# Queries and values by seven block products, and two parts of the modulation summed later

## The chip, the cores and the metric

The kernel runs on one core of a Trainium2 chip. What counts is the device time of one execution in microseconds, as the median of several runs. The times shown are 3068.38 us as median of three runs (3064.83 to 3071.08). The profile is of one further execution, which took 3069.78 us with a span of 3067.9 us from the first to the last instruction.

## The reference

Two residual blocks follow each other on 256 tokens of width 2048, all in float32. The change touches the first one only:

```
mod   = silu(c) @ w_mod + b_mod              # 6 parts of 2048
hl    = modulate(rms_norm(x), mod[0], mod[1])    # 256 tokens
hc    = modulate(rms_norm(ctx), ...)             # 256 context tokens
zl    = hl @ w_in + b_in        # conv, gating (su, sv), q, k, v, 3 gates
zkv   = hc @ w_in[k, v] + b_in
y_na  = neighbourhood_attention(q, k, v, kc, vc, rpb)
x     = x + mod[2] * (g_conv*y_conv + g_sgu*y_sgu + g_att*y_att) @ w_o
h2    = modulate(rms_norm(x), mod[3], mod[4])
x     = x + mod[5] * (square(relu(h2 @ w_ff1 + b1)) @ w_ff2 + b2)
```

q needs the 256 tokens only; k and v need the tokens and the context. `mod[2]` to `mod[5]` are vectors of 2048: each is a sum over 2048 rows of `w_mod` weighted by `silu(c)`. The second block has its own projections, a dilated attention and three recurrences, and is not touched.

## The kernel before

**Engines and queues.** The order of the work is written out by hand for each engine, in one function per engine, with semaphores between them. TensorE (PE) does all products, VectorE (DVE) the element work, ScalarE (ACT) activations and copies out of PSUM. SyncE's queue (SP) loads the weights into a ring of four slots of 1 MB, in the order of the table `STREAM`; a slot is loaded again once PE has released it. The queue of GpSimd (POOL) loads the chunks of `w_mod`.

**Two kinds of product.** A stationary product (`one_slot`, line 473) goes through the slot's 128 columns: sixteen matmuls with 256 tokens (q, su, sv) or 512 (k). The other kind is `pair` (line 493): the block of 256 columns by 256 tokens is cut in halves on the three axes, and seven products of the halves replace eight. Three of the seven read the ring directly. The other four read sums of weight blocks, which DVE makes in `pair_differences` and `pair_sums` (lines 1773, 1754, 1785) and announces on `weight_sums`; `quarter_sums` (line 1815 on) makes the sums of the inputs, announced on `input_sums`. `add_products` (lines 1797 to 1806, five operations) puts the seven results together and frees the two PSUM banks. There is one buffer `TX` for the weight sums: the differences of the next pair wait for `differences_used`, its first sum for the first bank of the pair before to be full, its second sum for the second bank, which is full when PE has done the pair. The three gates' projections and most of the feed-forward layers are done so.

**The stages around the change.** After the opening PE does su, sv, q, k and v, then gate_conv, the output projections of conv and sgu, gate_sgu and gate_att (16 pairs, called gate_sgu below), out_att, the output projection, ff1 and ff2. In q each of eight slots is a stationary product; in k too, with layer norm sums of the other branches between; v is done with the tokens as the stationary operand, 128 products of 512 columns (line 770). The attention itself is spread through the gate stages.

**The modulation.** Each of parts 3 to 6 (here called first to fourth, `mod_columns(0)` to `(3)`) is summed by DVE over sixteen chunks of 128 rows by 2048 columns (`add_chunk`, line 1918) into `MACC`, and a small product of PE (`mod_sum`, line 684) sums it over the partitions; it waits on `mod_added`. Two buffers hold chunks, and the table `CHUNK_AT` says beside which slot a chunk's load may start. All 64 chunks are added between the end of the opening and the end of v: twenty between the 24 groups of eleven convolution taps (line 1970), the others around the layer norms and during v.

Of the kernel before, what the change touches and what calls it, by code (L numbers as in the profile page):

```python
# [18 lines left out]
ALU = mybir.AluOpType  # L19
# [37 lines left out]
for _n, _pack in enumerate(PACKS):  # L57
# [10 lines left out]
    ("q", "w_in", WQ, 2, 16, 128), ("k", "w_in", WK, 2, 16, 128), ("v", "w_in", WV, 2, 4, 512),  # L68
# [38 lines left out]
def second_layer(q):  # L107
# [7 lines left out]
CHUNK_PARTS = tuple(g for g in range(24) if g not in (10, 11, 12, 20))  # L115
CHUNK_AT = (-4, -3, 0, 1, 2, 3, *(3 + g for g in CHUNK_PARTS), *(x - 12 for x in (39, 39, 39, 40, 40, 40, 42, 42, 42, 43, 43, 43, 44, 44, 44, 45, 45, 45,
            46, 46, 46, 47, 48, 48, 48, 48, 49, 49, 49, 49, 50, 50, 50, 50, 51, 51, 51, 51)))
assert len(CHUNK_AT) == 64

# [42 lines left out]
def program(nc, dram, out):  # L162
    ctx = ExitStack()
    with ctx:
# [17 lines left out]
        glw = sb("glw", [P, KT, 32])  # L182
        small = sb("small", [P, 16])
# [43 lines left out]
        MACC_ROWS = at(34032, KT, 4, 32)  # L227
# [18 lines left out]
        XS, X21 = at(24592, 7, HT, P), at(13328, HT, P)  # L246
        TB, TB0 = [at(o, 4, HT, P) for o in (4096, 14352)]
# [11 lines left out]

        TO = [at(2048 * e, 4, 4, P) for e in range(2)]  # L260
# [106 lines left out]
        def _(sp):  # L367
# [58 lines left out]
        def _(pe):  # L426
# [57 lines left out]
            def pair(p, x, tb, mid=None, first=0, tokens=False):  # L484
# [21 lines left out]
                for i, t, o in ((0, 3, psum[:, b, P:2 * P]), (1, 5, psum[:, b, 2 * P:3 * P]),  # L506
# [6 lines left out]
                    if i == 1:  # L513
                        mm.then_inc(sem("differences_used"), n["differences_used"].up())
                    elif i == 2:
                        mm.then_inc(sem(full("dve", a)), n[full("dve", a)].up())
                    elif i == 3:
                        mm.then_inc(sem(full("dve", b)), n[full("dve", b)].up())

# [159 lines left out]
            def mod_sum(b):  # L679
# [3 lines left out]
                for i in range(4):  # L683
                    mm = pe.matmul(psum[32 * i:32 * i + 32, b, :], ones[:, 0:32], MACC_ROWS[:, :, i, :], start=True,
                                   stop=True)
# [15 lines left out]

            def ahead_of_sv(q, k):
                if q == 5 and k == 0:
                    mod_sum(7)
# [54 lines left out]
            for half in range(2):  # L759
                for t in range(4):  # L760
                    take(4 * half + t, "act")
                for s in range(4):
                    w = slot(s, 512)
                    for k in range(4):
                        for t in range(4):
                            if half == 0 and s == k == 1 and t == 0:
                                mod_sum(7)
                            elif half == 1 and s == 3 and k == 2 and t == 0:
                                mod_sum(3)
                            mm = pe.matmul(psum[:, 4 * half + t, :], H[:, 4 * s + k, t * P:(t + 1) * P], w[:, k, :],  # L770
                                           start=(s == k == 0), stop=(s == k == 3))
                            if t == k == 0:
                                leave(mm, s)
                            if s == k == 3:
                                mm.then_inc(sem(full("act", 4 * half + t)), n[full("act", 4 * half + t)].up())


# [44 lines left out]
            pe.wait_ge(sem("input_sums"), n["input_sums"].next())  # L822
# [109 lines left out]
            for q in range(64):  # L932
                hidden_slot(q)

# [248 lines left out]
        def _(act):  # L1183
# [113 lines left out]
            def beside_su(q):  # L1297
# [7 lines left out]
                elif q < 6:  # L1305
# [7 lines left out]
                    if q == 5:  # L1313
                        settled("ctx_normed", range(4, 6))

            beside("su", tiles("su", ZU, ACT.Gelu_apprx_tanh, (cols, COL["b_in"] + SU // P)), beside_su)
            beside("sv", tiles("sv", ZV, ACT.Gelu_apprx_tanh, (cols, COL["b_in"] + SV // P)), alone)
            settled("uv_ready")
            act.wait_ge(sem("bq_ready"), n["bq_ready"].next())
            beside("q", lambda i, s: A(turned(one(NQ, i * 4 + s)), psum[:, s, 0:T].rearrange("p (r c) -> p r c", c=GRID),  # L1320
                                       ACT.Identity, scale=0.125, bias=bq[:, ds(i * 4 + s, 1)]), alone)

            def beside_k(q):
                if q == 4:

                    load(kept[0], at(0, 4096), "load_x_out")
# [14 lines left out]
            for half in range(2):  # L1341
                for t in range(4):
                    b = 4 * half + t
                    act.wait_ge(sem(full("act", b)), n[full("act", b)].next())
                    A(NV[:, t, half * 512:half * 512 + 512], psum[:, b, :], ACT.Copy).then_inc(
                        sem(free("act", b)), n[free("act", b)].up())
            settled("qkv_ready", range(8))
# [243 lines left out]
        def _(pool):  # L1591
# [39 lines left out]
            for j in range(64):  # L1631
# [18 lines left out]

            pool.wait_ge(sem("gates_added"), n["gates_added"].next())
# [23 lines left out]
            pool.dma_start(kept[1], at(36080, 4096)).then_inc(sem("load_tables_out"), 16)  # L1675
# [1408 lines left out]
```

## Time and profile before

| | |
|---|---|
| median of three runs | 3068.38 us |
| the profiled execution | 3069.78 us, span 3067.9 us |
| PE busy | 3016.4 us, 98% |
| DVE busy | 2056.0 us, 67% |
| ACT, POOL busy | 332.4 us, 63.2 us |
| mean granted clock of TensorE | 0.998 |
| q stage (from about 324 us), v stage | eight slots up to 379.5 us; 500.35 to 612.67 us |
| gate_sgu and gate_att, last pairs | up to 1066.0 us |
| ff1 pairs, second layer | from 1246.9 us; from 1626.3 us |

An engine's busy share is a mean over stages with different limits. PE is busy almost throughout from 170 us on, so the time of a stage is what PE has to do in it plus what it waits, and DVE's idle time in a stage says how much more it could take there before PE feels it. A matmul in float32 shows as two records in the trace, so 16 products are x32.

### The profile page before, as it was taken

How to read it: one execution, taken by the hardware profiler on the slowest of the kernel's cores; microseconds unless marked ns; L12 is line 12 of the kernel's file. 1: busy time of each engine (PE TensorE's matmuls, PEld its weight loads, DVE VectorE, ACT ScalarE, POOL GpSimd, SP SyncE). 2: the span in 40 equal slices, each digit the busy share in tenths (PEclk: the TensorE clock that was granted, in tenths of full speed). 3: DMA queues.
4: the chain of work that ended last, by engine and by line, in shares of the span. 5: the costliest groups of instructions: out<-in, count | busy, mean ns of one | idle time of the engine just before them, and what ended most of it. 6: DMA issues, size and time to landing. Idle time of an engine off the chain costs nothing.

```text
span 3067.9 us, 50576 instructions
## 1 busy us (share of the span) xinstructions
PE 3016.4 (98%) x22131; PEld 2727.2 (89%) x22143; DVE 2056.0 (67%) x3101; ACT 332.4 (11%) x651; POOL 63.2 (2%) x121
## 2 busy tenths in 40 slices
PE   6899999999999999999999999999999999999998
PEld 3588844499999999999999999999999998898998
DVE  1039975567876577766756777877667566996665
ACT  1011000023220000111110000001012102001010
POOL 0000000120000000000000000000000000000000
PEclk9999999999999999999999999999999999999999
DMA  8899977664445555755555555565444654553443
GB/s 290 289 310 297 295 241 287 227 186 137 138 138 165 182 176 165 190 168 165 192 173 165 169 166 165 166 174 172 148 145 146 206 174 124 154 140 110 124 151 111
DMA packets 580137, 561.45 MB, mean 183 GB/s; under 512 B 24317, under 2 KB 548176, under 8 KB 570445
## 3 DMA queue, kind: packets, MB, share of 16 engines
q1 hardware_dynamic: 550368, 466.65, 49.7%
q0 software_dynamic: 11552, 80.90, 7.1%
q10 hardware_dynamic: 17997, 10.67, 1.2%
q8 instruction: 175, 2.87, 0.4%
q14 instruction: 45, 0.37, 0.0%
HBM read 549.66 MB, written 8.51 MB: 182 GB/s over the span
## 4 chain that ended last, share of the span: by engine, by line
PE 73%; DVE 1%; issue 0%; ACT 0%; DVEq 0%; ACTq 0%
PE psum L493 36%; PE psum L473 15%; PE psum L571 2%; PE psum L901 2%; PE psum L891 2%; PE psum L903 2%; PE psum L896 2%; PE psum L893 2%; PE psum L902 2%; PE psum L888 2%; PE psum L536 2%; PE psum L946 1%; PE psum L529 1%; PE psum L583 1%; PE psum L1076 0%; PE psum L1089 0%
## 5 line engine op out<-in xcount | busy, mean ns | idle before, releaser
L473 PE MATMUL psum<-arena,ring 128*128 128x256 f32 (+2 forms) x3200 | 756.1, 397 | 0.9 <-ACTq L1191 0.9
L473 PEld LDWEIGHTS psum<-arena,ring 128*128 128x128 f32 x3200 | 604.2, 190 | 138.8 <-issue 63.5
L493 PE MATMUL psum<-arena 128*128 128x128 f32 x6144 | 702.8, 275 | 0.3 <-DVE arena L1785 0.3
L493 PEld LDWEIGHTS psum<-arena 128*128 128x128 f32 x6144 | 694.4, 192 | 7.2 <-issue 6.2
L493 PE MATMUL psum<-arena,ring 128*128 128x128 f32 x4224 | 486.1, 275 | 0.0
L493 PEld LDWEIGHTS psum<-arena,ring 128*128 128x128 f32 x4224 | 479.1, 192 | 0.7 <-issue 0.5
L1773 DVE TENSOR_TENSOR arena<-ring 128x2048 f32<-128x2048 f32 x96 | 220.0, 2292 | 278.4 <-PE psum L493 276.0
L1918 DVE SCALAR_TENSOR_TENSOR arena<-arena,cvec 128x2048 f32<-128x2048 f32 x60 | 141.0, 2350 | 78.6 <-DMA arena<-w_mod 77.7
L1754 DVE TENSOR_TENSOR arena<-ring,arena 128x1024 f32<-128x1024 f32 (+1 forms) x184 | 178.3, 969 | 5.7
L1754 DVE TENSOR_TENSOR arena<-arena 128x512 f32<-128x512 f32 (+7 forms) x267 | 141.2, 529 | 16.3 <-DVE arena L2696 5.7
L2553 DVE TENSOR_TENSOR arena<-ring 128x1024 f32<-128x1024 f32 x64 | 78.4, 1225 | 90.3 <-PE psum L888 89.5
L1785 DVE TENSOR_TENSOR arena<-ring,arena 128x1024 f32<-128x1024 f32 x96 | 117.6, 1225 | 3.6 <-DVE arena L1754 0.3
L770 PE MATMUL psum<-ring,arena 128*128 128x512 f32 x256 | 110.6, 593 | 1.0 <-ACT arena L1339 1.0
L633 PE MATMUL psum<-arena,ring 128*128 128x256 f32 x448 | 104.8, 389 | 6.7 <-DMA ring<-w_in 4.3
L633 PEld LDWEIGHTS psum<-arena,ring 128*128 128x128 f32 x448 | 85.3, 194 | 28.9 <-DMA ring<-w_in 16.6
L770 PEld LDWEIGHTS psum<-ring,arena 128*128 128x128 f32 x256 | 48.4, 190 | 63.2 <-issue 63.2
L891 PE MATMUL psum<-arena,ring 128*128 128x128 f32 x512 | 99.0, 275 | 0.0
L901 PE MATMUL psum<-arena 128*128 128x128 f32 x512 | 99.0, 275 | 0.0
L893 PE MATMUL psum<-arena,ring 128*128 128x128 f32 x512 | 99.0, 275 | 0.0
L902 PE MATMUL psum<-arena 128*128 128x128 f32 x512 | 99.0, 275 | 0.0
L903 PE MATMUL psum<-arena 128*128 128x128 f32 x512 | 99.0, 275 | 0.0
L888 PE MATMUL psum<-arena,ring 128*128 128x128 f32 x512 | 99.0, 275 | 0.0
(345 smaller groups left out, 3211.8 us busy)
## 6 DMA issues: line engine op xcount, KB each, us to landing
ring<-w_ff SPq DMA_DIRECT2D x128, 1024.0 KB, 5.7
ring<-w_in SPq DMA_DIRECT2D x88, 1024.0 KB, 7.3
arena<-w_mod POOLq DMA_DIRECT2D x64, 1024.0 KB, 6.6
ring<-ab_w_in SPq DMA_DIRECT2D x56, 1024.0 KB, 5.7
ring<-cd_w_in SPq DMA_DIRECT2D x48, 1024.0 KB, 5.8
ring<-w_mod SPq DMA_DIRECT2D x32, 1024.0 KB, 7.6
ring<-w_in SPq DMA_DIRECT2D x32, 512.0 KB, 4.8
ring<-w_o SPq DMA_DIRECT2D x16, 1024.0 KB, 5.8
```

The source lines that it names most:

```text
L473: mm = pe.matmul(psum[:, s, m * N:(m + 1) * N], w[:, k, m * P:(m + 1) * P], x(k)[:, 0:N], start=(j == 0), stop=(j == kt - 1))
L493: return pe.matmul(o, z, w, **kw) if tokens else pe.matmul(o, w, z, **kw)
L633: mm = pe.matmul(psum[:, b, m * T:(m + 1) * T], w[:, k, m * P:(m + 1) * P], HL[:, 4 * g + k, :], start=False, stop=g == 3 and k == 3 and m ...
L770: mm = pe.matmul(psum[:, 4 * half + t, :], H[:, 4 * s + k, t * P:(t + 1) * P], w[:, k, :], start=(s == k == 0), stop=(s == k == 3))
L888: mm = pe.matmul(psum[:, a, 0:P], quarters(s, 0, 0)[:, j], HID[:, 8 * g + 2 * j, 0:P], start=False, stop=False)
L891: pe.matmul(psum[:, a, P:2 * P], quarters(s, 1, 0)[:, j], HID[:, 8 * g + 2 * j + 1, 0:P], start=False, stop=False)
L893: pe.matmul(psum[:, b, 3 * P:4 * P], quarters(s, 1, 1)[:, j], h[:, 3, j, :], start=False, stop=False)
L901: pe.matmul(psum[:, b, 0:P], w[:, 3, j, :], HID[:, 8 * g + 2 * j + 1, P:2 * P], start=False, stop=False)
L902: pe.matmul(psum[:, b, P:2 * P], w[:, 0, j, :], h[:, 0, j, :], start=False, stop=False)
L903: mm = pe.matmul(psum[:, b, 2 * P:3 * P], w[:, 1, j, :], h[:, 2, j, :], start=False, stop=g == 7 and j == 3)
L1754: step(v.tensor_tensor(o, a, b, op))
L1773: step(v.tensor_tensor(tb[:, 0:2], w[:, :, :, 1].rearrange("p i f c -> p f i c"), w[:, :, 0].rearrange("p i m c -> p m i c"), ALU.subtract))
```

## The change

q and v are done in the pair form. q is four pairs with the input sums `SQ0`, made after tap group 15, and its weight sums stand between tap groups 15 to 19; DVE adds up the products into `STAGEA`, and ACT writes q from there. v is four weight pairs, each with both halves of the tokens (the sequence and the context; `pair_of_two`), 14 products a pair; the context's sums are in `HCS` and `HCS3`. Only 32 chunks are added before the end of v. The third part (`mod_columns(2)`) is summed in gate_sgu pairs 5 to 14 from its own loads into buffers that the attention has left (`add_gate_chunk`), the fourth in ff1 pairs 19 to 29 and the first five double slots of the second layer, in half chunks (`add_late`). The write of x to memory starts earlier, ahead of sv.

```diff
-    ("q", "w_in", WQ, 2, 16, 128), ("k", "w_in", WK, 2, 16, 128), ("v", "w_in", WV, 2, 4, 512),
+    ("q", "w_in", WQ, 2, 2, 256), ("k", "w_in", WK, 2, 16, 128), ("v", "w_in", WV, 2, 2, 256),
...
-CHUNK_PARTS = tuple(g for g in range(24) if g not in (10, 11, 12, 20))
+CHUNK_PARTS = tuple(range(0, 16, 2))
+CHUNK_AT = (-4, -3, 0, 1, 2, 3, *(3 + g for g in CHUNK_PARTS), 25, 25, 26, 27, 28, 29, 30, 31, 32, 33, 34, 35, 36, 36,
+            37, 37, 38, 38)
...
+            def pair_of_two(p, xs, tb):
+
+                s0 = 2 * (p % 2)
+                for h, x in enumerate(xs):
+                    a, b = 2 * h, 2 * h + 1
+                    if h == 0:
+                        for s in (s0, s0 + 1):
+                            slot(s, 2 * P)
+                    take(a, "dve")
+                    take(b, "dve")
...
+                    if h == 0:
+                        pe.wait_ge(sem("weight_sums"), n["weight_sums"].next())
+                    for i, t, o in ((0, 3, psum[:, b, P:2 * P]), (1, 5, psum[:, b, 2 * P:3 * P]),
+                                    (2, 4, psum[:, a, 2 * P:3 * P]), (3, 2, psum[:, b, 0:P])):
+                        for j in range(HT):
+                            mm = pe.matmul(o, x(t, j), tb[:, i, j, :], start=(j == 0), stop=(j == HT - 1))
...
-            beside("sv", HL, "act", alone, ahead=ahead_of_sv)
-            beside("q", HL, "act", alone)
+            beside("sv", HL, "act", alone)
+            pe.wait_ge(sem("input_sums"), n["input_sums"].next())
+            for p in range(4):
+                pair(p, halves(HL, SQ0), TX)
...
+            pe.wait_ge(sem("input_sums"), n["input_sums"].next())
+            for p in range(4):
+                pair_of_two(p, (halves(HL, SM), context_quarters), TX)
+                if p == 1:
+                    mod_sum(7)
...
             for p in range(16):
                 pair(p, halves(HL, SB), TX, mid=lambda p=p: attend(26 + 2 * p))
                 attend(27 + 2 * p)
+                if p == 14:
+                    mod_sum(7, GATE_ROWS)
...
             for q in range(64):
                 hidden_slot(q)
+                if q == 11:
+                    mod_sum(7, LATE_ROWS)
...
-            for j in range(64):
+            for j in range(32):
...
+            pool.wait_ge(sem("att_ready"), 1)
+            for k in range(KT):
+                pool.wait_ge(sem(f"chunk{k % 2}_used"), n[f"chunk{k % 2}_used"].next())
+                pool.dma_start(GCHUNK[k % 2], w[:, k, 4096 + 2 * D:4096 + 3 * D]).then_inc(sem(f"load_chunk{k % 2}"), 16)
...
+                if g == 15:
+                    quarter_sums(HL, SQ0, "input_sums")
+                    v.wait_ge(sem("load_x_out"), 16)
+                    w = pair_differences("q", 0, TX)
+                    pair_sums(0, w, TX)
+                elif 17 <= g < 21:
+                    p = g - 17
+                    if p < 3:
+                        w = pair_differences("q", p + 1, TX)
+                        pair_sums(p + 1, w, TX)
+                    if p >= 2:
+                        v.wait_ge(sem("stage_taken"), p - 1)
+                    pairs_added(p, STAGEA)
...
+            for p in range(4):
+                for h in range(2):
+                    v.wait_ge(sem("stage_taken"), 4 + 2 * p + h - 1)
+                    if h == 1:
+                        w = pair_differences("v" if p < 3 else "gate_conv", (p + 1) % 4, TX, used=fast[0] + p + 1)
+                        pair_sums((p + 1) % 4, w, TX, bank=2)
+                    add_products(h, 2 * h, 2 * h + 1, STAGEA)
+                    v.sem_inc(sem("pair_ready"), n["pair_ready"].up())
+                    if p < 2:
+                        chunk = chunks(2)
+                if p == 1:
+                    mod_columns(1, 7)
+                    v.sem_inc(sem("mod_done"), n["mod_done"].up())
...
+                elif 5 <= p < 9:
+                    add_gate_chunk(p - 5)
+                elif 9 <= p < 15:
+                    add_gate_chunk(2 * p - 14)
+                    add_gate_chunk(2 * p - 13)
                 elif p == 15:
+                    mod_columns(2, 7, at(18432, KT, 32))
                     single_sums("out_att", 0)
...
-                elif p == 25:
-
-                    TT(gain[:, 1, :], mod[:, 80:96, 0], col("b_ff2", 0, KT), ALU.mult)
...
+                if p >= 19:
+                    add_late(p - 19)
...
+                if i < 5:
+                    add_late(11 + i)
+                elif i == 6:
+                    mod_columns(3, 7, at(36080, KT, 32))
```

The order of the instructions moves with it. On PE, in v, before: L770 are the v products, L684 the modulation sum of the third part.

```order
L770 MATMUL psum<-ring,arena 128x512 [waits load_slot1]
L770 MATMUL psum<-ring,arena 128x512 x3
L684 MATMUL psum<-arena,ones 32x512 [waits bank7_read_by_dve,mod_added]
L684 MATMUL psum<-arena,ones 32x512 x3
L770 MATMUL psum<-ring,arena 128x512 x12
```

And in the changed kernel, where L537 and L547 are the products of the second weight pair with the context half (the latter on the weight sums), and L721 the modulation sum of the second part:

```order
L537 MATMUL psum<-ring,arena 128x128 [waits bank3_read_by_dve,bank2_read_by_dve]
L537 MATMUL psum<-ring,arena 128x128 x15
L537 MATMUL psum<-ring,glw 128x128 x4
L537 MATMUL psum<-ring,arena 128x128 x4
L547 MATMUL psum<-arena 128x128 x32
L721 MATMUL psum<-arena,ones 32x512 [waits bank7_read_by_dve,mod_added]
L721 MATMUL psum<-arena,ones 32x512 x3
L537 MATMUL psum<-ring,arena 128x128 [waits bank0_read_by_dve,bank1_read_by_dve,load_slot1,load_slot0]
```

The modulation sum now stands behind a whole weight pair and ahead of the next. On DVE, at the same place of v, before: the last of the chunks of the third part (L1918) and what follows them.

```order
L1918 SCALAR_TENSOR_TENSOR arena<-arena,cvec 128x2048 [waits load_chunk0,chunk1_used]
L1918 SCALAR_TENSOR_TENSOR arena<-arena,cvec 128x2048 [waits load_chunk1,chunk0_used]
L1929 TENSOR_TENSOR arena<-psum,diagonal 128x512 [waits chunk1_used,bank7_full_for_dve]
L1932 TENSOR_REDUCE mod<-arena 128x16 [waits bank7_read_by_dve]
L1754 TENSOR_TENSOR mod<-mod,cols 128x16 [waits vector_step]
```

And in the changed kernel: the weight sums of the third weight pair (L1823, L1802, L1837), the adding up of the seven products (L1849 to L1858), the last two chunks (L1970), the reading of PE's sum (L2008).

```order
L1823 TENSOR_TENSOR arena<-ring 128x2048 [waits load_slot1,load_slot0,differences_used,stage_taken,chunk1_used]
L1802 TENSOR_TENSOR arena<-ring,arena 128x1024 [waits bank2_full_for_dve,vector_step]
L1837 TENSOR_TENSOR arena<-ring,arena 128x1024 [waits bank3_full_for_dve,vector_step]
L1849 COPY arena<-psum 128x128 [waits bank2_full_for_dve,weight_sums]
L1851 TENSOR_TENSOR arena<-arena,psum 128x2x128 [waits vector_step]
L1802 TENSOR_TENSOR arena<-arena,psum 128x2x128 [waits bank3_full_for_dve,bank2_read_by_dve]
L1857 TENSOR_TENSOR arena<-arena,psum 128x128 [waits vector_step]
L1858 TENSOR_TENSOR arena<-arena,psum 128x2x128
L1970 SCALAR_TENSOR_TENSOR arena<-arena,cvec 128x2048 [waits vector_step,bank3_read_by_dve,load_chunk0]
L1970 SCALAR_TENSOR_TENSOR arena<-arena,cvec 128x2048 [waits load_chunk1,chunk0_used]
L2008 TENSOR_TENSOR arena<-psum,diagonal 128x512 [waits chunk1_used,bank7_full_for_dve]
```

The last two chunks stand behind a weight sum that waits for a full bank. In gate_sgu, on DVE, pair 14 of the changed kernel has the two chunks of the third part (L1983) between the weight sums and the adding:

```order
L1802 TENSOR_TENSOR arena<-ring,arena 128x1024 [waits bank0_full_for_dve,vector_step]
L1837 TENSOR_TENSOR arena<-ring,arena 128x1024 [waits bank1_full_for_dve,vector_step]
L1983 SCALAR_TENSOR_TENSOR arena<-arena,cond 128x2048 [waits load_chunk0,stage_taken,weight_sums]
L1983 SCALAR_TENSOR_TENSOR arena<-arena,cond 128x2048 [waits load_chunk1,chunk0_used]
L1849 COPY arena<-psum 128x128 [waits chunk1_used,bank0_full_for_dve]
```

Before, the adding followed the weight sums there with nothing between.

## Rows read from the trace of the kernel before

**Rows 1.** The page's busy us of each engine, share of the span, instructions.

```profile
PE 3016.4 (98%) x22131; PEld 2727.2 (89%) x22143; DVE 2056.0 (67%) x3101; ACT 332.4 (11%) x651; POOL 63.2 (2%) x121
```

**Rows 2.** PE's waits: what waited for whom, us in total, times, longest.

```profile
PE psum L770 <- ACT arena L1339: 1.0, 1, 1.0
...
PE psum L732 <- DVE arena L2036: 0.5, 1, 0.5
```

**Rows 3.** Timeline of PE, sv to gate_conv: start us, us, line, operation.

```profile
302.32 1.06 PE L684 MATMUL psum<-arena,ones 128*32 128x512 f32 x8
303.32 89.97 PE L473 MATMUL psum<-arena,ring 128*128 128x256 f32 x384
...
393.56 13.90 PE L473 MATMUL psum<-arena,ring 128*128 128x512 f32 x32
...
500.35 17.40 PE L770 MATMUL psum<-ring,arena 128*128 128x512 f32 x40 [0.98 <-ACT arena L1339]
...
612.67 5.52 PE L493 MATMUL psum<-arena,ring 128*128 128x128 f32 x48
618.03 7.31 PE L493 MATMUL psum<-arena 128*128 128x128 f32 x64
625.18 5.52 PE L493 MATMUL psum<-arena,ring 128*128 128x128 f32 x48
```

**Rows 4.** Timeline of DVE in the tap groups, same columns.

```profile
235.72 4.44 DVE L1970 SCALAR_TENSOR_TENSOR arena<-arena,taps 128x256 f32<-128x256 f32 x11
240.07 2.35 DVE L1918 SCALAR_TENSOR_TENSOR arena<-arena,cvec 128x2048 f32<-128x2048 f32 x1
242.46 4.44 DVE L1970 SCALAR_TENSOR_TENSOR arena<-arena,taps 128x256 f32<-128x256 f32 x11
```

**Rows 5.** Timeline of DVE beside k: one centring, first and last operation.

```profile
395.40 0.42 DVE L1995 TENSOR_SCALAR arena<-psum 128x256 f32<-128x256 f32 x1
...
400.51 3.67 DVE L1987 TENSOR_REDUCE arena<-arena 128x256 f32<-128x2048 f32 x1
```

**Rows 6.** Timeline of DVE: the first of four input sums.

```profile
586.98 1.22 DVE L1815 TENSOR_TENSOR arena<-arena 128x1024 f32<-128x1024 f32 x1
```

**Rows 7.** Timeline of DVE, gate_conv: weight sums and adding of a pair.

```profile
621.90 2.29 DVE L1773 TENSOR_TENSOR arena<-ring 128x2048 f32<-128x2048 f32 x1 [14.05 <-PE psum L493]
...
625.49 1.23 DVE L1785 TENSOR_TENSOR arena<-ring,arena 128x1024 f32<-128x1024 f32 x1
626.75 0.29 DVE L1797 COPY arena<-psum 128x128 f32<-128x128 f32 x1
...
634.41 2.29 DVE L1773 TENSOR_TENSOR arena<-ring 128x2048 f32<-128x2048 f32 x1 [5.81 <-PE psum L493]
```

**Rows 8.** Windows (PE, PEld, DVE, ACT, POOL busy, PEclk, DMA, GB/s); PE's timeline.

```profile
49.00:50.00 1.00, 0.37 (x4) 0.34 (x4) 0.82 (x3) 0.00 (x0) 0.00 (x0) 0.50 1.05 395
...
3062.00:3064.00 2.00, 0.00 (x0) 0.00 (x0) 0.00 (x0) 0.37 (x1) 0.00 (x0) 0.63 1.01 399
...
50.58 6.08 PE L633 MATMUL psum<-arena,ring 128*128 128x256 f32 x16 [1.21 <-DVE arena L1880]
...
57.81 3.62 PE L633 MATMUL psum<-arena,ring 128*128 128x256 f32 x16
...
3058.28 0.61 PE L1177 MATMUL psum<-ones,arena 128*128 128x1 f32 x4 [0.18 <-DVEq L3038]
```

**Rows 9.** DMA: packets, MB and share by queue; issues with us to landing.

```profile
q1 hardware_dynamic: 550368, 466.65, 49.7%
q0 software_dynamic: 11552, 80.90, 7.1%
...
arena<-w_mod POOLq DMA_DIRECT2D x64, 1024.0 KB, 6.6
```

**Rows 10.** Timeline of DVE behind ff1 pair 19 and in the second layer.

```profile
1510.29 2.29 DVE L1773 TENSOR_TENSOR arena<-ring 128x2048 f32<-128x2048 f32 x1 [1.43 <-PE psum L493]
...
1665.03 1.23 DVE L2553 TENSOR_TENSOR arena<-ring 128x1024 f32<-128x1024 f32 x1 [3.58 <-PE psum L888]
```

More of the change, by code:

```diff
@@ L754, in _, with context_quarters @@
             beside("su", HL, "act", beside_su)
-            beside("sv", HL, "act", alone, ahead=ahead_of_sv)
-            beside("q", HL, "act", alone)
+            beside("sv", HL, "act", alone)
+            pe.wait_ge(sem("input_sums"), n["input_sums"].next())
+            for p in range(4):
+                pair(p, halves(HL, SQ0), TX)
             pe.wait_ge(sem("ctx_normed"), n["ctx_normed"].next())
             beside("k", H, "act", beside_k, N=2 * T, ahead=ahead_of_k)
[L759 to L775, printed above, removed]
+            def context_quarters(t, j):
+                if t < 3:
+                    return GATE[:, 2 * j + (t > 0), P * (t == 2):P * (t == 2) + P]
+                if t < 6:
+                    return HCS[t - 3][:, j, :]
+                k, z = [(k, z) for k, z in HCS3 if k <= j][0 if j < 4 else 1 if j < 7 else 2]
+                return z[:, j - k, :]
+            pe.wait_ge(sem("input_sums"), n["input_sums"].next())
[3 more added lines that the diff above has]
+                    mod_sum(7)
             def scores(p):
@@ L1319, in _ @@
             act.wait_ge(sem("bq_ready"), n["bq_ready"].next())
[L1320 to L1321 removed]
+            for p in range(4):
+                act.wait_ge(sem("pair_ready"), n["pair_ready"].next())
+                for m in range(2):
+                    i = 4 * (p % 2) + 2 * m
+                    z = STAGEA[:, i:i + 2, :].rearrange("p a t -> p (a t)")
+                    ins = A(turned(NQ[:, 2 * p + m, :]), z.rearrange("p (r c) -> p r c", c=GRID), ACT.Identity, scale=0.125,
+                            bias=bq[:, 2 * p + m:2 * p + m + 1])
+                ins.then_inc(sem("stage_taken"), n["stage_taken"].up())
             def beside_k(q):
[L1324 to L1326 removed]
                 if q == 1 or q == 4:
@@ L1340, in _ @@
                                        bias=cols[:, ds(i * 4 + (COL["b_in"] + WK // P + s), 1)]), beside_k)
[L1341 to L1347, printed above, removed]
+            for p in range(4):
+                for h in range(2):
+                    act.wait_ge(sem("pair_ready"), n["pair_ready"].next())
+                    for m in range(2):
+                        ins = A(NV[:, 2 * h:2 * h + 2, (2 * p + m) * P:(2 * p + m + 1) * P],
+                                STAGEA[:, 4 * h + 2 * m:4 * h + 2 * m + 2, :], ACT.Copy)
+                    ins.then_inc(sem("stage_taken"), n["stage_taken"].up())
+            act.wait_ge(sem("stage_taken"), n["stage_taken"].now())
+            settled("qkv_ready")
             act.wait_ge(sem("conv_normed"), n["conv_normed"].next())
```

156 lines of the change are left out of this document (107 added, 49 removed).

## The prediction

> **What bounds the kernel now.** I read the busy shares first [rows 1]: TensorE (PE) works 98% of the span, VectorE (DVE) 67%. The reader is to see that only two things count: what PE has to do, and where it has to wait. The waits of PE come second: nearly all lie in the first 160 us, in the loads of the opening, which the change leaves alone; from 170 us to the end they are single waits of at most 1 us, and those in the stages touched are the two of [rows 2]. Third comes PE's timeline of the stages that the change rewrites [rows 3], since it gives the price of a stage without a model. Then DVE's timeline in the same places [rows 4 to 7], because DVE makes what the new products read: where PE now overtakes DVE, PE waits.
>
> **The products themselves.** The row that starts at 303.32 holds eleven column blocks of 256 tokens and one k block of 512; the k block alone is 13.90 us, so one block of 256 is (89.97 - 13.90) / 11 = 6.92 us [rows 3]. The eight q blocks are 55.3 us. Afterwards q is four pairs. A pair of the existing kind goes from 612.67 to 625.18, 12.51 us, 5.36 of them before it reads the DVE's weight sums [rows 3]. Four pairs are 50.0 us: 5.3 us less. The v stage lasts from 500.35 to 612.67, with two modulation sums of 1.00 us (as 302.32 to 303.32) inside: 110.3 us. Afterwards it is four weight pairs times two token halves, eight times 12.51 = 100.1 us: 10.2 us less. Together 15.5 us of PE work. The four modulation sums stay four.
>
> **What DVE must have ready for q.** Ahead of q stand 24 groups of taps. A group of 11 taps takes 240.07 - 235.72 = 4.35 us and a chunk of the modulation 242.46 - 240.07 = 2.39 us [rows 4]. Groups 1 to 15 and the seven chunks left between them end at 235.7 + 15 x 4.35 + 7 x 2.39 = 317.7. The input sums are four operations of 1.22 (4.9 us with their gaps) [rows 6], the differences 2.3 and the two sums 2.5 [rows 7]: ready at 322.6 and 327.4. PE ends sv at 302.32 + 3 x 6.92 = 323.1, the modulation sum being gone from there, and reads the first weight sums at 328.4. No wait, by a margin of 0.5 us. For the second pair DVE does two more groups first: 327.4 + 8.7 + 0.1 + 4.8 = 341.0; PE wants them at 323.1 + 12.5 + 5.4 = 341.0. I take 0.3 us of waiting (0 to 1.5). Pairs three and four have a group each per 12.5 us (4.4 + 4.8 + 1.9 = 11.1 us) and cost nothing. q ends at 373.4 instead of 379.5; DVE, after its last groups, at about 381.4 instead of 377.6.
>
> **The layer norms beside k.** DVE needs two tile sums (3.7 each), two chunks and the centring (395.40 to 404.18, 8.8 us) [rows 5]: 381.4 + 7.4 + 4.8 + 8.8 = 402.4. PE wants it after two k blocks and a small sum, 373.4 + 13.75 + 0.4 + 13.75 = 401.3: 1.1 us of waiting (0 to 3). Against this the two waits of [rows 2], 0.5 and 1.0 us, should go: the chunks ahead of the gating end 5 us earlier, and the new v products wait for banks that were read long ago. Together +0.1 us net.
>
> **The modulation sum in the middle of v.** This is where the gain is spent. In the changed order PE does the two halves of the second weight pair and then the modulation sum, which waits for the last two chunks. DVE's order is: second weight sum, five operations that add up the seven products, chunk, chunk. The weight sum waits for the last bank, which is full only when PE has ended the pair. So the chunks cannot begin before PE stands still. In the trace PE's next pair starts at 625.18 [rows 3] and the first adding operation at 626.75, 1.57 us later; the five end 5.81 us before 634.41, at 628.60, 1.85 us [rows 7]. Two chunks are 4.8 us. PE waits 1.57 + 1.85 + 4.8 = 8.2 us. In the kernel before the chunks stood far ahead of this sum, and no wait is seen. Both chunks' loads are issued when their buffers come free, some 9 to 11 us ahead, against 6.6 us to landing [rows 9], so I add nothing; above, a late load could add 3.
>
> **The same in gate_sgu.** Behind pair 14 stands the third part's sum. DVE does the weight sum and then chunks 14 and 15 ahead of the adding: 1.57 + 4.8 = 6.3 us of waiting (range 6 to 9). Elsewhere in the stage there is room: in a pair without attention work DVE is idle 5.81 us between the adding and the next differences (634.41 is one, the last pairs of gate_sgu are alike) [rows 7], and two chunks take 4.8.
>
> **What the pauses do to the clock.** At the end of the kernel the last matmuls end at 3058.9, and the granted clock is 0.63 on average over 3062 to 3064, so it fell from 2.4 to 1.2 GHz some four us after PE went idle; in the opening it was at 0.50 at 49 to 50 us after sparse work, and the sixteen matmuls that follow took 6.08 us where the next sixteen took 3.62 [rows 8]. Both new pauses are longer than that stretch, so I take one such loss each: 2 x 2.5 = 4.9 us (0 to 7; none if the level holds across the pause). The Trainium skill, TensorE: Matmul & The Clock Gate (Why this matters for your kernels), says that an idle stretch between bursts of matmuls puts the clock back to half: by that rule the sum is the one with the 4.9 us, without it 4.9 less. Where the trace shows such a pause it agrees [rows 8].
>
> **The feed-forward layers.** Each late step is two operations on 1024 columns, 1.25 us each (half of a chunk's 2.35 and its overhead), 2.5 us. Pairs 19 to 21 leave DVE 1.43 us free each [rows 10], so it falls 1.1 us further behind on each, 3.2 in all; the weight sums are ready 1.6 us after a pair starts and read 5.4 us after, a margin of 3.8. No wait, and pair 22 has room to recover. In the second layer DVE is free 3.58 us in every other slot [rows 10]; 2.5 fit. The sum of the fourth part stands seven slots behind its last chunk. Cost 0, and 3 at most if that cover is gone.
>
> **The sum.** -15.5 + 0.3 + 1.1 - 1.5 + 8.2 + 6.3 + 4.9 = +3.8 us. Two of the four modulation sums only move to later stages. Against its own profiled execution (3069.78 us, span 3067.9) that gives 3073.6; the median of the runs shown is 1.4 us lower, so I forecast 3072. Its own range is 3067 to 3077: the clock's 0 to 7, the small waits' 0 to 4.5.
>
> **Rivals.** (1) The pauses are there but the clock holds: 3072 - 4.9 = 3067. For it: a pause of 6 to 8 us inside dense work is in no row. Against it: [rows 8]. (2) PE does not wait at the two sums, because DVE is ahead by more than I think: then 14.5 and 4.9 us go, 3072 - 19.4 = 3053. For it: every other sum before was covered. Against it: the order of waits in the changed program, in which the weight sum stands ahead of the chunks. (3) The other side: in gate pairs 9 to 14 the DMA queues carry two slots and two chunks, 4.19 MB in 12.5 us, 335 GB/s. The shares say that this just fits: SP's queue moved 466.65 MB in 49.7% of the span, 306 GB/s, and POOL's 80.90 MB in 7.1%, 371 GB/s [rows 9], so 6.9 + 5.7 = 12.5 us of DMA per 12.5. At the 306 for both, 13.7 us, six pairs fall 7 us behind. It decides once a chunk takes longer than the 10 us between its buffer's release and its use, for then DVE's weight sums are late too: 3072 + 7 = 3079, slower. For it: no stage has shown such a rate for long. Against it: the ring is loaded two pairs ahead and swallows several us. (4) The products don't pay as reckoned (operands in other places, a slower kind of product): half of the 15.5 gone, 3080.
>
> **Chances.** The forecast 0.50; rival 1, 0.17; rival 2, 0.13; rival 3, 0.13; rival 4, 0.07. No change is within 0.2%, about what a measurement of this kernel can tell, 3062.2 to 3074.5. Of the forecast 0.38 lies inside and 0.12 above; rival 1 inside with 0.17; rival 2 below; of rivals 3 and 4 0.18 above and 0.02 inside; 0.03 of rival 1 and the forecast I move below for waits that turn out shorter. So faster 0.16, same 0.54, slower 0.30. The range of 3059 to 3080 leaves out rival 2 and little above.
>
> **What would show it.** Right: in the waits of PE, one of about 8 us and one of about 6 on the modulation sums' line, each ended by DVE's chunk addition; q in four times 12.5 us and v in eight times 12.5; granted clock near 0.5 for some us behind each pause; PE's busy time 14 to 15 us less, apart from the slow stretches. Wrong: no such waits (rival 2), a clock of 1.00 behind them (rival 1), waits of DVE for chunk loads in gate_sgu (rival 3), pairs of more than 12.6 us (rival 4), or waits at the feed-forward pairs 20 to 22, where I count none.

## The result and the profile after

The changed kernel takes 3070.81 us (median of 20 runs, 3065.99 to 3075.77), the kernel before 3065.36 us (median of 20, 3059.96 to 3071.08): ratio 1.0018, 95% interval 1.0011 to 1.0025. It is slower by 5.4 us: the ratio is just inside the 0.2% that I had called no change, and its interval reaches past it. The forecast was 3072. Its profiled execution took 3074.06 us, span 3072.3, against 3069.78 and 3067.9.

The page of the changed kernel, busy us of each engine, as [rows 1]:

```profile
PE 3008.1 (98%) x22963; PEld 2784.4 (91%) x22975; DVE 2127.5 (69%) x3212; ACT 332.9 (11%) x659; POOL 71.6 (2%) x137
```

PE is busy 8.3 us less in spite of slow stretches, and yet the span is 4.4 us longer. The waits of PE in the changed kernel, from 300 to 1070 us, columns as in [rows 2]:

```profile
PE psum L721 <- DVEq L1975: 8.2, 1, 8.2
PE psum L721 <- DVEq L1988: 7.2, 1, 7.2
PE psum L627 <- DVE arena L2082: 1.7, 1, 1.7
...
PE psum L497 <- DVE arena L1837: 0.5, 1, 0.5
PE psum L765 <- DVE arena L2130: 0.5, 1, 0.5
```

Line 721 is the modulation sum. The two long waits are the two pauses forecast at 8.2 and 6.3. Line 627 is the layer norm sum beside k, line 765 the gating products; the wait at v's first banks [rows 2] is gone.

PE's timeline of the same kernel, q to the first pair of gate_conv and the end of the gates, as [rows 3]:

```profile
320.58 5.62 PE L497 MATMUL psum<-arena,ring 128*128 128x128 f32 x48
...
339.24 7.41 PE L497 MATMUL psum<-arena 128*128 128x128 f32 x64 [0.52 <-DVE arena L1837]
...
371.50 13.90 PE L477 MATMUL psum<-arena,ring 128*128 128x512 f32 x32
...
493.27 5.52 PE L537 MATMUL psum<-ring,arena 128*128 128x128 f32 x48
...
551.70 1.93 PE L721 MATMUL psum<-arena,ones 128*32 128x512 f32 x8 [8.24 <-DVEq L1975]
553.57 7.45 PE L537 MATMUL psum<-ring,arena 128*128 128x128 f32 x48
...
605.52 5.52 PE L497 MATMUL psum<-arena,ring 128*128 128x128 f32 x48
...
1053.55 1.94 PE L721 MATMUL psum<-arena,ones 128*32 128x512 f32 x8 [7.22 <-DVEq L1988]
1055.42 7.41 PE L497 MATMUL psum<-arena,ring 128*128 128x128 f32 x48
...
1069.81 2.84 PE L566 MATMUL psum<-arena,ring 128*128 128x128 f32 x24
```

The reader is to see the price of the stages: q from 320.58 to 371.50 (50.9 us), v from 493.27 to 605.52 (112.3 us: eight times 12.51, a sum of 1.0, the wait of 8.24 and 2.8 of slow clock), and the same work at two speeds: the 24 products (48 records) that open a pair take 5.52 us, behind a pause 7.45 and 7.41; the sum of 1.06 us [rows 3] takes 1.93 and 1.94. So each of these two pauses costs (7.45 - 5.52) + (1.93 - 1.06) = 2.8 us more than its length.

The stages against those forecast, all from PE's timelines. The start of q in the kernel before is 303.32 + 3 x 6.92 = 324.06 [rows 3]; its q ends at 379.5.

| stretch | before | forecast | after | what differs from the forecast |
|---|---|---|---|---|
| q | 55.4 | 50.4 | 50.9 | wait of 0.52 instead of 0.3; pairs 0.1 longer |
| k, to the start of v | 119.9 | 120.5 | 121.8 | layer norm wait 1.7, not 1.1; gating wait stayed |
| v | 113.3 | 111.8 | 112.3 | clock 2.8 instead of 2.5 |
| gate_conv to out_att | 453.3 | 463.1 | 464.3 | wait 7.2, not 6.3; clock |
| q to out_att | 741.9 | 745.7 | 749.2 | |

(The forecast column is my terms put on the column before: q -5.3 + 0.3, k +1.1 - 0.5, v -10.2 - 1.0 (one sum fewer) - 1.0 + 8.2 + 2.5, gates +6.3 + 2.5 + 1.0.) The stretch from q to out_att is what I go by below beside the medians, because the opening is left out of it: PE reaches q in the experiments that share this opening anywhere from 316.3 to 320.7 us, a spread larger than several of the effects. The changed kernel reaches q at 320.58, 3.5 us sooner than the kernel before; 1.0 of that is the modulation sum that no longer stands in sv. Behind out_att the two kernels differ by 0.6 us, 2001.9 and 2002.5.

### The profile page after: what moved, and what is told of

The parts are those of the page before. It is cut to its first block, busy times and chain, and to the rows that moved or that the text cites. A ratio compares the mean times of both kernels' runs of the same rounds, so it can differ in the third digit from the quotient of the medians.

```text
span 3072.3 us, 52418 instructions
## 1 busy us (share of the span) xinstructions
PE 3008.1 (98%) x22963; PEld 2784.4 (91%) x22975; DVE 2127.5 (69%) x3212; ACT 332.9 (11%) x659; POOL 71.6 (2%) x137
## 4 chain that ended last, share of the span: by engine, by line
PE 87%; DVE 7%; DMA 5%; issue 0%; ACT 0%; DVEq 0%; SPq 0%; ACTq 0%; POOLq 0%
PE psum L497 39%; PE psum L477 17%; DVE arena L2049 3%; PE psum L573 2%; PE psum L670 2%; DMA arena<-w_mod 2%; PE psum L566 2%; PE psum L608 2%; PE psum L919 2%; PE psum L932 2%; PE psum L922 2%; PE psum L933 2%; PE psum L924 2%; PE psum L927 2%; PE psum L934 2%; PE psum L547 2%
## 5 line engine op out<-in xcount | busy, mean ns | idle before, releaser
L497 PE MATMUL psum<-arena 128*128 128x128 f32 x6400 | 732.1, 275 | 0.8 <-DVE arena L1837 0.8
L497 PEld LDWEIGHTS psum<-arena 128*128 128x128 f32 x6400 | 723.3, 192 | 7.9 <-issue 6.2
L477 PE MATMUL psum<-arena,ring 128*128 128x256 f32 (+2 forms) x2944 | 700.7, 398 | 0.6 <-ACTq L1224 0.6
L477 PEld LDWEIGHTS psum<-arena,ring 128*128 128x128 f32 x2944 | 555.6, 190 | 131.1 <-issue 62.7
L497 PE MATMUL psum<-arena,ring 128*128 128x128 f32 x4416 | 510.2, 276 | 0.0
L497 PEld LDWEIGHTS psum<-arena,ring 128*128 128x128 f32 x4416 | 502.5, 193 | 2.3 <-issue 1.7
L1823 DVE TENSOR_TENSOR arena<-ring 128x2048 f32<-128x2048 f32 x104 | 238.4, 2292 | 240.7 <-PE psum L497 212.3
L1802 DVE TENSOR_TENSOR arena<-ring,arena 128x1024 f32<-128x1024 f32 (+1 forms) x192 | 188.1, 980 | 6.0
L1802 DVE TENSOR_TENSOR arena<-arena 128x512 f32<-128x512 f32 (+6 forms) x269 | 143.6, 534 | 16.4 <-DVE arena L2816 5.7
L1837 DVE TENSOR_TENSOR arena<-ring,arena 128x1024 f32<-128x1024 f32 x104 | 127.4, 1225 | 3.6
L670 PEld LDWEIGHTS psum<-arena,ring 128*128 128x128 f32 x448 | 86.2, 196 | 29.1 <-DMA ring<-w_in 14.8
L919 PE MATMUL psum<-arena,ring 128*128 128x128 f32 x512 | 99.1, 275 | 0.0
L933 PE MATMUL psum<-arena 128*128 128x128 f32 x512 | 99.0, 275 | 0.0
L924 PE MATMUL psum<-arena,ring 128*128 128x128 f32 x512 | 99.0, 275 | 0.0
L922 PE MATMUL psum<-arena,ring 128*128 128x128 f32 x512 | 99.0, 275 | 0.0
L932 PE MATMUL psum<-arena 128*128 128x128 f32 x512 | 99.0, 275 | 0.0
L934 PE MATMUL psum<-arena 128*128 128x128 f32 x512 | 99.0, 275 | 0.0
L1849 DVE COPY arena<-psum 128x128 f32<-128x128 f32 x140 | 40.8, 291 | 83.4 <-PE psum L547 41.9
L2049 DVE SCALAR_TENSOR_TENSOR arena<-arena,taps 128x256 f32<-128x256 f32 x240 | 96.4, 479 | 0.9
L573 PE MATMUL psum<-arena 128*128 128x128 f32 x768 | 89.7, 275 | 0.0
```

The costliest lines, as they stand in the source:

```text
L477: mm = pe.matmul(psum[:, s, m * N:(m + 1) * N], w[:, k, m * P:(m + 1) * P], x(k)[:, 0:N], start=(j == 0), stop=(j == kt - 1))
L497: return pe.matmul(o, z, w, **kw) if tokens else pe.matmul(o, w, z, **kw)
L670: mm = pe.matmul(psum[:, b, m * T:(m + 1) * T], w[:, k, m * P:(m + 1) * P], HL[:, 4 * g + k, :], start=False, stop=g == 3 and k == 3 and m ...
L919: mm = pe.matmul(psum[:, a, 0:P], quarters(s, 0, 0)[:, j], HID[:, 8 * g + 2 * j, 0:P], start=False, stop=False)
L922: pe.matmul(psum[:, a, P:2 * P], quarters(s, 1, 0)[:, j], HID[:, 8 * g + 2 * j + 1, 0:P], start=False, stop=False)
L924: pe.matmul(psum[:, b, 3 * P:4 * P], quarters(s, 1, 1)[:, j], h[:, 3, j, :], start=False, stop=False)
```

## The experiments

All kernels below ran beside the kernel before, 3064.9 us on both occasions; the changed kernel itself, 3070.8, ran beside a median of 3065.4.

**Which order of sum and pair.** Each of the first three keeps all products and moves the long waits away: the modulation sum is put behind later work of PE, so that DVE adds the last chunks while PE does products. e_both does it in both places, e_v in v alone, e_gate in gate_sgu alone.

```diff
             for p in range(4):
-                pair_of_two(p, (halves(HL, SM), context_quarters), TX)
-                if p == 1:
-                    mod_sum(7)
+                pair_of_two(p, (halves(HL, SM), context_quarters), TX, (lambda: mod_sum(7)) if p == 2 else None)
...
-                if p == 14:
+                if p == 15:
                     mod_sum(7, GATE_ROWS)
...
                 elif p == 15:
-                    mod_columns(2, 7, at(18432, KT, 32))
                     single_sums("out_att", 0)
...
             gate_pairs("gate_sgu", 16, 26, later_taken)
+            mod_columns(2, 7, at(18432, KT, 32))
```

(The function given to the pair is called between its two token halves. e_v is the upper part, e_gate the rest.)

> The changed kernel with both sums moved to where DVE has long done the chunks: the second part's sum behind the first half of the third weight pair of v (12.5 us later), the third part's behind gate_sgu's pair 15, and DVE reads it after that pair. Theory (the two waits of 8.24 and 7.22 us and twice 2.8 us of slow clock behind them ate the gain): all 21.0 us come back, 3070.8 - 21.0 = 3049.8 us against 3065.4 before, ratio 0.995; no wait over 2 us behind the opening, granted clock 1.00 throughout v and gate_sgu. Rival (DVE or the chunk loads are behind there anyway, and the waits only show at the first place where PE asks): PE waits at the next weight sums or banks instead, 3063 to 3071 us.

Measured: 3049.05 us (3046.80 to 3050.53, 5 runs), ratio 0.9949 (0.9937 to 0.9961). PE's timeline of e_both at the two sums:

```profile
546.01 7.31 PE L547 MATMUL psum<-arena 128*128 128x128 f32 x64
553.25 1.06 PE L723 MATMUL psum<-arena,ones 128*32 128x512 f32 x8
...
1045.15 1.07 PE L723 MATMUL psum<-arena,ones 128*32 128x512 f32 x8
1046.15 2.94 PE L568 MATMUL psum<-arena,ring 128*128 128x128 f32 x24
```

Neither sum waits, and both are at full speed; of the waits of PE between q and out_att only the small ones are left, the longest 1.7 us at the layer norms. Without the pauses and their clock (8.24 + 7.22 + 2 x 2.8 = 21.1 us) the medians should be 21.1 apart; they are 21.8, and the stretch from q to out_att is shorter by 21.3 (749.23 - 727.97). The kernel with the seven-product arithmetic, slower than the one before as it stood, is 0.5% faster than it once its sums stand one half pair, or one pair, later. DVE's timeline of e_both shows why half a pair is enough:

```profile
544.21 4.74 DVE L1970 SCALAR_TENSOR_TENSOR arena<-arena,cvec 128x2048 f32<-128x2048 f32 x2
554.39 0.69 DVE L2008 TENSOR_TENSOR arena<-psum,diagonal 128x512 f32<-128x512 f32 x1 [5.44 <-PE psum L723]
```

The chunks end at 548.95, 4.3 us before PE comes to the sum.

> Only the sum in v is moved, behind the first half of the third weight pair. Theory: the wait of 8.24 us and its slow clock of 2.8 us go, the one in gate_sgu stays with 7.2 + 2.8: 3070.8 - 11.0 = 3059.8 us. Rival (what is gained in v is waited for again in the gate stages, by the bias loads or DVE): 3068 to 3071 us.

Measured: 3059.82 us (3054.89 to 3067.65, 11 runs), ratio 0.9982 (0.9973 to 0.9992).

> Only the sum in gate_sgu is moved, behind pair 15. Theory: 7.22 + 2.8 us go, the wait in v stays: 3070.8 - 10.0 = 3060.8 us. If the two are independent, this and the run with only v moved add up to the run with both. Rival (the loads of the third part's chunks keep DVE late in gate_sgu, so that PE waits at out_att instead): 3067 to 3071 us.

Measured: 3060.18 us (3057.06 to 3065.85, 12 runs), ratio 0.9990 (0.9982 to 0.9999). The long wait that each keeps, from the waits of PE, first of e_v:

```profile
PE psum L723 <- DVEq L1988: 6.3, 1, 6.3
```

and of e_gate:

```profile
PE psum L721 <- DVEq L1975: 8.2, 1, 8.2
```

The pause in v is worth 11.0 us by the medians, that in gate_sgu 10.6, together 21.6, near the 21.8 of e_both: neither covers the other. The interval of each is some 3 us wide to either side, so the stretch says more. From q to out_att, e_v takes 736.3 us (1053.10 - 316.80), 12.9 less than the changed kernel, and e_gate 739.3 (1055.60 - 316.34), 10.0 less; together 22.9, where both moved give 21.3. The two are thus not quite independent. PE's timeline of e_v behind the pause that it keeps:

```profile
1037.80 1.94 PE L723 MATMUL psum<-arena,ones 128*32 128x512 f32 x8 [6.26 <-DVEq L1988]
1039.67 6.45 PE L497 MATMUL psum<-arena,ring 128*128 128x128 f32 x48
```

The pause is 1.0 us shorter than in the changed kernel, and so is the loss behind it: (6.45 - 5.52) + (1.94 - 1.06) = 1.8 us instead of 2.8. In e_gate the loss behind the pause in v is 2.5 (the 24 products take 7.13 us). Four pauses of 6.3 to 8.3 us thus cost 1.8 to 2.8 us each beyond their length; what sets the figure within that, no run here shows.

**Pause or clock.** e_fill keeps both waits but has PE do products that nobody reads ahead of them: 18 and 15 of 128 by 256.

```diff
-            def mod_sum(b, rows=MACC_ROWS):
+            def mod_sum(b, rows=MACC_ROWS, busy=0):
...
-                pe.wait_ge(sem("mod_added"), n["mod_added"].next())
                 take(b, "dve")
+                for i in range(busy):
+                    pe.matmul(psum[:, b, 0:T], ones[:, :], HL[:, i % KT, :], start=True, stop=True)
+                pe.wait_ge(sem("mod_added"), n["mod_added"].next())
```

> The changed kernel with both waits left where they are, but ahead of each PE does products that nobody reads (18 and 15 of 256 columns into the bank of the sum, 0.43 us each, 7.8 and 6.5 us), so PE is busy instead of idle while DVE adds the chunks. Theory (2.8 us are lost behind each pause because the clock fell in it): the granted clock stays at 1.00, the waits shrink to 0.5 and 0.7 us, nothing else changes: 3070.8 - 5.6 = 3065.2 us. Rival (the loss behind the pauses is a restart of another kind, or the slow level doesn't matter): 3070 to 3071 us.

Measured: 3064.77 us (3062.02 to 3068.05, 11 runs), ratio 1.0001 (0.9993 to 1.0010): 6.0 us less than the changed kernel, with both sums at their old places in the order. Windows of the changed kernel around its two pauses (columns as in [rows 8]):

```profile
545.00:547.00 2.00, 0.00 (x0) 0.00 (x0) 1.77 (x6) 0.20 (x1) 0.00 (x0) 1.00 1.10 352
547.00:549.00 2.00, 0.00 (x0) 0.00 (x0) 2.00 (x1) 0.52 (x2) 0.00 (x0) 0.55 0.69 218
549.00:551.70 2.70, 0.00 (x0) 0.00 (x0) 2.56 (x2) 0.00 (x0) 0.00 (x0) 0.50 0.02 6
551.70:553.00 1.30, 1.30 (x8) 0.20 (x8) 0.00 (x0) 0.00 (x0) 0.00 (x0) 0.50 0.02 6
...
556.00:558.00 2.00, 2.00 (x14) 2.00 (x13) 0.00 (x0) 0.00 (x0) 2.00 (x4) 0.64 0.33 66
558.00:560.00 2.00, 2.00 (x21) 2.00 (x20) 0.00 (x0) 0.00 (x0) 2.00 (x4) 1.00 0.81 140
...
1054.00:1057.00 3.00, 3.00 (x15) 1.58 (x8) 2.70 (x6) 0.91 (x2) 0.00 (x0) 0.50 0.00 0
1057.00:1060.00 3.00, 3.00 (x20) 3.00 (x19) 2.84 (x5) 0.00 (x0) 0.00 (x0) 0.64 0.00 0
1060.00:1062.00 2.00, 2.00 (x21) 2.00 (x20) 0.00 (x0) 0.00 (x0) 0.00 (x0) 1.00 0.00 0
```

and of e_fill:

```profile
540.00:560.00 20.00, 19.52 (x141) 17.41 (x140) 9.99 (x13) 0.72 (x2) 5.28 (x8) 1.00 0.46 135
1040.00:1060.00 20.00, 20.00 (x151) 18.11 (x150) 13.36 (x17) 0.91 (x2) 0.00 (x0) 1.00 0.53 178
```

PE stops at 543.46 us (551.70 - 8.24). In the changed kernel the granted clock is still 1.00 (2.4 GHz) from 545 to 547 us, falls while PE stands, and is 0.50 (1.2 GHz) at the end of the pause and while PE starts again; it is 1.00 again only in the windows from 558 and, behind the second pause, from 1060 us. In e_fill it is 1.00 in both windows. In e_fill's timeline the products fill the first pause but for 0.47 us:

```profile
540.30 7.94 PE L720 MATMUL psum<-arena,ones 128*128 128x256 f32 x36
548.72 1.07 PE L723 MATMUL psum<-arena,ones 128*32 128x512 f32 x8 [0.47 <-DVEq L1977]
```

So the two terms are separate: 15.5 us of waiting, which another order gives back and filling does not, and 5.6 of slow clock, given back by keeping PE at work (6.0 by the medians, 5.8 from q to out_att, where small shifts of the waits are counted too: the sum in gate_sgu came 0.8 us sooner, that in v and the gating products 0.3 us later each). The Trainium skill, TensorE: Matmul & The Clock Gate (Why this matters for your kernels), says that an idle stretch between bursts puts the clock back to half. These two pauses of 8.2 and 7.2 us agree: the granted clock fell to 0.50 in both.

**The layer norm wait.** e_ln is e_both with the centring ahead of two chunks instead of behind them.

```diff
             centre = layer_norm_sums(ZV, SQ, 4)
-            chunk = chunks(2)
             centre()
+            chunk = chunks(2)
```

> Both sums moved, and beside k DVE does the centring of the layer norm ahead of two chunks instead of behind them. Theory: PE's wait of 1.7 us for the squares goes, since DVE is ready 4.8 us earlier, and nothing waits for the two chunks before the sum that PE does 16 us later: 3049.05 - 1.7 = 3047.4 us. Rival (PE is then held at the next sum or the next norm): 3049 us.

Measured: 3050.26 us (3048.97 to 3052.81, 5 runs), ratio 0.9950 (0.9938 to 0.9963). By the times this is inconclusive: no gain over e_both, both intervals nearly the same. The trace of e_ln:

```profile
398.42 0.59 PE L629 MATMUL psum<-arena,ones 128*128 128x256 f32 x2
```

The wait of 1.7 us is gone; 0.5 came back at the gating products (0.7 instead of 0.2). From q to out_att e_ln takes 1046.04 - 319.60 = 726.4 us, e_both 1046.15 - 318.18 = 728.0: the 1.5 us are there in the stage. In that profile PE reached q 1.4 us later, which takes most of them back. Whether the times would show them with more runs was not tried.

**What the products are worth.** e_noq and e_nov are e_both with q, or v, done as in the kernel before. Core of e_noq:

```diff
-            pe.wait_ge(sem("input_sums"), n["input_sums"].next())
-            for p in range(4):
-                pair(p, halves(HL, SQ0), TX)
+            beside("q", HL, "act", alone)
```

> Both sums moved, and q undone: eight stationary blocks of 256 tokens again, without input sums, weight sums and adding on DVE. Theory (the q products are worth 55.3 - 50.0 = 5.3 us, less what DVE's 32 us more work costs at its two small waits, 0.8 and 1.7 us): 3049.05 + 5.3 - 2.5 = 3051.9 us. Rival A (the pairs are worth what is counted and DVE's load costs nothing): 3054.4 us. Rival B (q brings nothing): 3049 us or less.

Measured: 3051.24 us (3050.62 to 3052.70, 5 runs), ratio 0.9953 (0.9940 to 0.9967). By the medians the seven products for q save 2.2 us net, not 5.3; with five runs each the two intervals overlap, so the times alone do not show it. The traces do: from q to out_att e_noq takes 730.4 us (1047.46 - 317.04; its q is the last eight of eighteen equal blocks between 247.97 and 372.29), e_both 728.0, so q's pairs save 2.4 net. In q they save 4.5 (55.3 against 50.9, in which the 0.5 of the second pair is counted), and beside k 1.9 is lost again, 1.7 of it the wait at the layer norms. PE's timeline of e_noq at the layer norms, without that wait:

```profile
400.19 0.59 PE L629 MATMUL psum<-arena,ones 128*128 128x256 f32 x2
```

Core of e_nov, in which v is 128 products of 512 columns again:

```diff
+            for half in range(2):
...
+                for s in range(4):
+                    w = slot(s, 512)
+                    for k in range(4):
+                        for t in range(4):
...
+                            mm = pe.matmul(psum[:, 4 * half + t, :], H[:, 4 * s + k, t * P:(t + 1) * P], w[:, k, :],
+                                           start=(s == k == 0), stop=(s == k == 3))
...
-            for p in range(4):
-                pair_of_two(p, (halves(HL, SM), context_quarters), TX, (lambda: mod_sum(7)) if p == 2 else None)
```

> Both sums moved, and v undone: 128 products of 512 columns with the tokens stationary again, the second part's sum ahead of their last eighth, no sums of the context, q still in pairs. Theory (v is worth 110.3 - 100.1 = 10.2 us and nothing of it is waited away): 3049.05 + 10.2 = 3059.3 us, up to 1 more for the wait at the first bank that v had before. Rival (part of it is lost to DVE or the ring): 3054 to 3057 us.

Measured: 3062.01 us (3056.28 to 3068.05, 11 runs), ratio 0.9990 (0.9981 to 0.9999). Doing v in pairs is worth 13.0 us by the medians. Timeline of PE in e_nov:

```profile
494.38 10.97 PE L816 MATMUL psum<-ring,arena 128*128 128x512 f32 x25 [0.98 <-ACT arena L1392]
...
605.52 5.52 PE L500 MATMUL psum<-arena,ring 128*128 128x128 f32 x48
...
1059.60 2.94 PE L571 MATMUL psum<-arena,ring 128*128 128x128 f32 x24
```

and in e_both:

```profile
490.63 5.52 PE L537 MATMUL psum<-ring,arena 128*128 128x128 f32 x48
...
591.87 5.52 PE L497 MATMUL psum<-arena,ring 128*128 128x128 f32 x48
```

With its first wait the v stage lasts 605.52 - (494.38 - 0.98) = 112.1 us in e_nov, and 591.87 - 490.63 = 101.2 in e_both: 10.9, of which 0.98 is the wait at the first banks and 9.9 the products, reckoned at 10.2. From q to out_att it is 738.9 (1059.60 - 320.74) against 728.0, the same 10.9. The 2 us by which the medians say more are not in this stretch, and the interval of e_nov (some 3 us to either side) allows them as noise. e_nov's profile came to q 2.6 us later than e_both's; no run tests whether the openings differ beyond chance.

| kernel | median us | q to out_att us |
|---|---|---|
| before | 3064.9 | 741.9 |
| after | 3070.8 | 749.2 |
| e_fill | 3064.8 | 743.5 (1060.70 - 317.25) |
| e_gate | 3060.2 | 739.3 |
| e_v | 3059.8 | 736.3 |
| e_nov | 3062.0 | 738.9 |
| e_noq | 3051.2 | 730.4 |
| e_both | 3049.1 | 728.0 |
| e_ln | 3050.3 | 726.4 |

## Why the prediction was right, and where its terms were off

The mechanism was right: the seven products give back some 15 us of PE work, and two sums that PE meets before DVE has its last chunks take 15.5 us of waiting and 5.6 us of clock. The sum was +3.8 us; in the stretch where it all happens it came out at +7.3, and by the medians at +5.4 (3.4 to 7.7 by the interval). Nearly every term of waiting came out larger than I took it. That the absolute figure hit closer has luck in it, twice. The forecast stood on the median of three runs, 3068.38, and over 20 runs the kernel before is at 3065.36. And in the profiles the changed kernel reached q 2.5 us sooner than by the one sum that left sv; no term of mine covers that, and no run shows whether the change or chance did it.

- **Products (-15.5).** Pairs of 12.51 us in v as reckoned; q 0.4 us longer than 50.0, apart from its wait. PE's busy time fell by 8.3 + 5.6 = 13.9 us apart from the slow stretches, a little under the 14 to 15 named. Rival 4 is excluded by e_nov and e_noq: 9.9 us for the products of v, 4.5 for q with its wait.
- **q's second pair (+0.3, 0 to 1.5).** 0.52. The first pair, where I gave a margin of 0.5 us, has no wait in the changed kernel; but in e_gate, whose opening ended first, PE waited 0.7 us there for the input sums, so that margin was about used up.
- **Layer norms (+1.1, 0 to 3).** 1.7, and not independent of the q edit: e_noq has neither this wait nor that of q.
- **The two waits of [rows 2] (-1.5).** Half wrong. The 1.0 at v's first banks went. The 0.5 at the gating products stayed 0.5. I had let DVE's earlier chunks move that place forward. In DVE's timeline of the changed kernel it is held by other things:

```profile
416.16 0.42 DVE L2090 TENSOR_SCALAR arena<-psum 128x256 f32<-128x256 f32 x1 [6.33 <-PE psum L627]
...
445.43 2.35 DVE L1970 SCALAR_TENSOR_TENSOR arena<-arena,cvec 128x2048 f32<-128x2048 f32 x1 [6.92 <-DMA arena<-w_mod]
...
450.33 0.69 DVE L2130 TENSOR_TENSOR arena<-psum,arena 128x512 f32<-128x512 f32 x1
```

The last centring starts when PE's own sum is done, so it moves with PE; and from there to the gating DVE stands 10.4 us in all for the loads of its last chunks (9.7 in the kernel before). My reading that from 170 us on no wait of PE is over 1 us was also wrong: there is one of 1.16 at 854 us and, beside k, one of 0.44. The changed kernel has both too (1.15 and 0.44), so the sum is not touched.
- **The sum in v (+8.2).** 8.24. DVE's timeline of the changed kernel there has all three parts:

```profile
540.02 2.29 DVE L1823 TENSOR_TENSOR arena<-ring 128x2048 f32<-128x2048 f32 x1 [3.02 <-PE psum L547]
...
544.87 0.29 DVE L1849 COPY arena<-psum 128x128 f32<-128x128 f32 x1
...
546.85 4.74 DVE L1970 SCALAR_TENSOR_TENSOR arena<-arena,cvec 128x2048 f32<-128x2048 f32 x2
```

PE's last product of the pair ends at 551.70 - 8.24 = 543.46; the weight sum that waited for its bank ends and the adding begins at 544.87 (1.41 us), the adding lasts to 546.85 (1.98), the chunks 4.74, and 0.11 passes before PE's sum starts.

- **The sum in gate_sgu (+6.3, 6 to 9).** 7.22, mis-sized by 0.9. The same view in the gates:

```profile
1046.73 1.23 DVE L1837 TENSOR_TENSOR arena<-ring,arena 128x1024 f32<-128x1024 f32 x1
1047.99 2.35 DVE L1983 SCALAR_TENSOR_TENSOR arena<-arena,cond 128x2048 f32<-128x2048 f32 x1
1051.09 2.35 DVE L1983 SCALAR_TENSOR_TENSOR arena<-arena,cond 128x2048 f32<-128x2048 f32 x1 [0.75 <-DMA arena<-w_mod]
```

The last chunk came 0.75 us late, and the weight sum ahead of the chunks started 0.40 us behind PE's last product (1046.33) instead of 0.15 as in v, since a late load had held DVE for 1.09 us in the pair before. I had bounded a late load at 3 us in v, and it fell here. In e_v, with both chunks on time, the same wait was 6.3, as reckoned.

- **The clock (+4.9, 0 to 7).** 2 x 2.8 = 5.6. The price was taken from sixteen matmul records of 256 columns in the opening [rows 8]; here it was 0.3 more, in e_gate the same and in e_v 0.7 less, so 2.5 was a fair size and not a constant. Rival 1 is refuted by the windows and by e_fill.
- **Rival 2 (no waiting).** Refuted by the two rows on line 721. Its figure of 3053, in turn, is what e_both gets near, once the order is changed.
- **Rival 3 (the rate of DMA).** It hardly showed. All chunk additions in the changed kernel from 900 to 1053 us, busy us and mean ns, then the idle time of DVE ahead of them:

```profile
L1983 DVE SCALAR_TENSOR_TENSOR arena<-arena,cond 128x2048 f32<-128x2048 f32 x15 | 35.3, 2352 | 2.3 <-DMA arena<-w_mod 1.8
```

Late chunks held DVE for 1.8 us in all, and PE paid for about 1.0 of it, at the sum. From 976 to 1039 us the queues moved 317 GB/s on average at a DMA share of 0.92: nearly full, and enough. The gates have no other new wait.
- **The feed-forward layers (0; 3 if the cover is gone).** 0: PE has no wait there that it did not have before. But the cover was nearly used. DVE in the changed kernel, the last weight sums of the first and fourth of four pairs in a row, and PE where it reads them:

```profile
1506.03 1.23 DVE L1837 TENSOR_TENSOR arena<-ring,arena 128x1024 f32<-128x1024 f32 x1
...
1546.15 1.23 DVE L1837 TENSOR_TENSOR arena<-ring,arena 128x1024 f32<-128x1024 f32 x1
```

```profile
1510.24 7.31 PE L497 MATMUL psum<-arena 128*128 128x128 f32 x64
...
1547.76 7.31 PE L497 MATMUL psum<-arena 128*128 128x128 f32 x64
```

The margin shrinks from 1510.24 - 1507.26 = 3.0 us to 1547.76 - 1547.38 = 0.4 us; I had reckoned 3.8 less 3.2, 0.6. In the pair behind it is 2.9 again.

## What to carry to other kernels

A product that sums up another engine's work has to stand behind enough independent products to cover the last of that work: read the order of the other engine from the semaphore it waits on, and put the sum far enough behind it (here half a pair more left 4.3 us to spare). Price such a pause in dense products as its length plus the slow clock behind it, here 1.8 to 2.8 us for pauses of 6.3 to 8.3. Where a change is worth a few us, compare the stretch that it touches in the traces as well as the medians; here the time at which the opening ended moved the total by as much.

## What the runs showed that was not expected

The opening, which no edit of these experiments touches, moves the start of q between 316.3 and 320.7 us from kernel to kernel, one profile each. And the saved products needed no further resource: e_both has the changed kernel's products, chunks and loads, and differs from it by the place of two sums, for 21.8 us (0.7%).
